# A forgetting bias built by VectorE, modulation sums placed inside dense matmuls, and later turns in a two-block transformer kernel

## Chip, cores and metric

One core of a Trainium2 chip runs the whole program. The metric is the device time of one execution in microseconds (us): 2219.46 us is the median of three runs of the kernel before (2216.54 to 2219.74).

## What is computed

256 tokens of width 2048 pass through two blocks, all in float32. The first block modulates its input with six vectors that come from a conditioning vector `c`, mixes tokens with a two-dimensional Fourier transform, and ends with a squared-ReLU MLP. The second has three kinds of attention heads over one wide projection and another MLP.

```python
# block 1
sh1, sc1, g1, sh2, sc2, g2 = split(silu(c) @ w_mod + b_mod)
h = rms_norm(x, g0) * (1 + sc1) + sh1
x = x + g1 * rms_norm(real(fft2(h per group of 256)) @ fnet_w_out, g1n)
x = x + g2 * rms_norm(relu(h2 @ w_mlp_in)**2 @ w_mlp_out, g3n)      # h2 = norm(x)*(1+sc2) + sh2
# block 2: xn = rms_norm(x) @ w_in gives gq gk gv gg ga fq fk fv fg ff mq mg
gla_o: gated linear attention, decay from ga        (8 heads of 64)
fox_o: logits = q.k/sqrt(d) + c[t] - c[s], causal, softmax, @ v;  c = cumsum(log_sigmoid(ff + b))
mem_o: softmax(mq . mk) @ mv over 256 memory tokens
x = x + (rms_norm([gla_o, fox_o, mem_o]) * gate) @ w_out
x = x + relu(rms_norm(x) @ w_up)**2 @ w_down
```

## The kernel before

**Weights.** Every large weight comes by a 512 KB transfer issued on SP's queue (`load`, L275, in the first part; `ring_group`, L312, later) into a slot of `raw`. The first part uses 12 slots, the rest 8. A float32 weight tile is split into a high part `wh` (ScalarE, `hi`, L949) and a low part `wl` (VectorE, `lo`, L1326), which is written over the raw tile. A "chunk" is one such tile: eight chunks make a group with its own PSUM banks. `T_chunk` (L443 to L449) puts out features on partitions, `N_chunk` (L461 to L463) tokens; a narrow T chunk has 24 matmuls of 256 columns, an N chunk 12 of 512. Matmuls of a chunk wait for `w_lo`; a slot is loaded again only when the chunk in it was used (`chunk_used`). Each engine runs its list of instructions in the order in which the program writes it, so where a step stands in that list is the schedule.

**Block 1, first stages.** The tiles of `w_mod` are multiplied by silu(c) in two ways: four at a time on TensorE (`mod_rows`, L509), or one at a time on VectorE (`gemv`, L1351), and `fold` (L1361) adds the first kind to the second. The result lies spread over 128 partitions in `acc`; `mod_sum` (L518) sums it over partitions with 16 matmuls (32 records) that have a column of ones, one column wide, as their moving operand. The order on TensorE is: the rows of sc1 mixed with Fourier transforms of token halves (`dft_tokens`, L538) and turns of `mem`; then eight T chunks and eight N chunks of the memory projection (`G_MEM`), with sh1's rows between them, `mod_sum(0, 2)` behind chunk 2, `dft_tokens(6)` behind chunk 3 and `dft_tokens(7)` behind the first N chunk; then `mod_sum(1, 7)` and eight `dft_features` (L606 to L608) with g1's rows; then 32 N chunks of `fnet_w_out` beside the gemvs of sc2.

**Start of the first MLP.** The rows of sh2 and the residual come first; `transposes(1, ...)` turns h, ScalarE writes it into `x1t` (L1091), `mod_sum(2, 6, (0,))` gives the first half of sh2, ScalarE adds it for the first two rounds of four tiles (L1099) and VectorE writes their low parts (`shifted_lo`, L1556). Rounds 2 and 3 need the second half: VectorE does the gemvs 24 to 31 with the split of chunk 3 before number 28, TensorE does `mod_sum(2, 7, (1,))` behind chunk 3 of the group (`shift_rest`), and rounds 2 and 3 go before the split of chunk 4. Chunk 4 needs round 2.

**Block 2.** Twelve groups of `w_in` (`WIN_GROUPS`: gq, gk, gv, gv, fq, fk, fv, mq, gg, gg, fg, mg; k = 0 to 11). Beside them, at fixed chunks i, stand the small attention steps. Nine decay levels (`att_level`, L799) serve the gated linear attention: in groups 2 to 5 the even one stands behind chunk 3 and the odd one behind chunk 6, and VectorE has to prepare each (`lvl_pre`, last step L1798). In group 8 `att_qk` computes the forgetting logits behind chunk 3: per head and token half one matmul of q and k, and two matmuls of rank 4 that add c[t] and subtract c[s]:

```python
last = mm(o, qq[:, hd, tb * P:(tb + 1) * P], kk[:, hd, :], start=tb == 0, stop=not fox, ...)      # L827
if fox:
    mm(o, fc[32:36, tb * P:(tb + 1) * P], sel[32:36, hd:hd + 1].to_broadcast([4, S]), ...)        # L830
    last = mm(o, nsel[32:36, hd, :], fc[32:36, :], start=False, stop=True, ...)                   # L832
```

VectorE then does `soft` (L1814 adds the causal mask, L1818 the row maxima, L1821 and L1823 the division; ScalarE the exponentials at L1236), which in its list stands behind the eight splits of group 8 (chunks 4 to 7 of group 8 and 0 to 3 of group 9). `att_turn` (L840) transposes the probabilities behind chunk 0 of group 9 and `att_pv` (L848) follows behind chunk 4. The same steps for the memory heads stand in groups 10 and 11, with no bias: their q·k matmuls are also at L827. `fc`, the running sum of the log forget gates, is ready on partitions 32 to 35 in group 1 (L1882).

Of the kernel before, what the change touches and what calls it, by code (L numbers as in the profile page):

```python
# [27 lines left out]
F32 = mybir.dt.float32  # L28
# [6 lines left out]
P = 128  # L35
# [34 lines left out]
def program(nc, x, c, w_mod, b_mod, norm_g, w_mlp_in, w_mlp_out, fnet_w_out, mem, attn_g, w_in, gla_w2, gla_b,  # L70
            fox_b, fox_qg, fox_kg, mem_g, w_mem_kv, mem_qg, mem_kg, out_g, w_out, mlp_g, w_up, w_down,
            k_ident, k_dft, k_mask, k_nsel, k_sel, k_levels, out):
    ctx = ExitStack()
    with ctx:
# [48 lines left out]
        rbc = at("rbc", [P, S], F32, O_RAW + RAW * 4 * KB)  # L123
        zt = at("zt", [P, 4, S], F32, O_RAW + RAW * 4 * KB + 1 * KB)
# [25 lines left out]
        nsel = at("nsel", [64, 4, P], F32, O_SLOT + 2 * KB)  # L150
# [6 lines left out]
        sel = const("sel", [64, 4], F32)  # L157
# [12 lines left out]
        mv_dram = nc.dram_tensor("mv_spill", [P, HALVES * GC], F32).ap()  # L170
        h_dram = nc.dram_tensor("h_spill", [P, HALVES * D], F32).ap()
# [181 lines left out]
        def _(pool):  # L353
# [59 lines left out]
            pool.dma_start(nsel[32:36, :, :], k_nsel.rearrange("p (a s) -> p a s", a=4)).then_inc(sem("att_const"), 16)  # L413
# [8 lines left out]
            pool.dma_start(flat(mv[:, :, :]), mv_dram).then_inc(sem("mkv_in"), 16)  # L422
            pool.wait_ge(sem("mem_pv"), 1)
# [5 lines left out]
        def _(pe):  # L429
            mm = nc.tensor.matmul  # L430

            def T_chunk(G, i, wide, s, split):
# [3 lines left out]
                for t in range(2):  # L436
                    kt = 2 * i + t
                    for j in range(4):
# [6 lines left out]
                        else:  # L445
# [3 lines left out]
                            last = mm(o, b, xt[:, kt, 0, :], start=False, stop=end, skip_group_check=True)  # L449
                last.then_inc(sem("chunk_used"), 1)  # L450
# [64 lines left out]
            def mod_sum(a, bank, halves=(0, 1)):  # L515

                for kt in range(8 * halves[0], 8 * halves[-1] + 8):
                    last = mm(ps[:, bank, kt:kt + 1], (acc[0], acc[1], acc2)[a][:, kt * P:(kt + 1) * P], ones[:, 0:1], start=True, stop=True,  # L518
                              skip_group_check=True)
                last.then_inc(sem("mod_mm"), 1)  # L520
# [9 lines left out]
            def dft_tokens(g):  # L530
                if g >= 2:
                    pe.wait_ge(sem("tok_out"), g if g == 7 else g - 1)
                for dt in range(2):
# [26 lines left out]
            mod_rows("sc1", C_SC1, 24, 0)  # L560
            pe.wait_ge(sem("rows_folded"), 2)
# [7 lines left out]
            for i in range(CH):  # L569
                if i % 2 == 0:  # L570
                    pe.wait_ge(sem("xt_ready"), 1 + i // 2)
                T_chunk(G_MEM, i, False, *early(i))
# [5 lines left out]
                if i == 2:  # L578
                    pe.wait_ge(sem("const_set"), 2)
                    mod_sum(0, 2)  # L580
            for i in range(CH):
# [4 lines left out]
                if i == 0:  # L586
                    dft_tokens(7)
# [265 lines left out]
            for k, (name, off) in enumerate(WIN_GROUPS):  # L853
                G = G_WIN + k
                bank_free(G)
                for i in range(CH):
# [17 lines left out]
                    if 2 <= k <= 5 and i == 6:  # L874
                        att_level(2 * (k - 2) + 1)
# [1147 lines left out]
```

## Time and profile before

| | |
|---|---|
| median of 3 runs | 2219.46 us |
| the profiled execution, its own time | 2221.41 us |
| its span, first to last instruction | 2219.7 us |
| TensorE matmul / weight load busy | 2156.7 us (97%) / 1823.6 us (82%) |
| VectorE / ScalarE / GpSimd busy | 1324.4 us (60%) / 972.6 us (44%) / 45.2 us (2%) |
| granted TensorE clock, mean | 0.98 of full |
| chain that ended last | TensorE 90%, VectorE 4%, DMA 3%, ScalarE 2% |

TensorE is busy nearly always, but busy does not mean fast: matmuls overlap in the pipeline, and where the granted clock is 0.50 each takes twice as long and counts as busy all the same. So three things are to be read of TensorE: its work, its waits and its clock. The execution's own time is 1.7 us over its span.

### The profile page before, as it was taken

To read this page: it belongs to the slowest core of one execution; us is meant where nothing else is said; L and a number is where in the kernel's file an instruction comes from. 1 tells how busy PE (TensorE), PEld (TensorE's weight loads), DVE (VectorE), ACT (ScalarE), POOL (GpSimd) and SP (SyncE) were. 2 spreads that over 40 slices of the span, in tenths; PEclk is the share of its full clock that TensorE was granted. 3 is DMA by queue.
4 is the path that set the end of the run, shared out by engine and by line. 5 is a ranking of instruction groups with operands and counts; after the bars stand their busy time and mean duration, and the time that the engine had idled before them with its cause. 6 is when DMAs were issued, how large, how long until landed. Compare 5 with 4: busy or idle time off the path is not lost.

```text
span 2219.7 us, 31332 instructions
## 1 busy us (share of the span) xinstructions
PE 2156.7 (97%) x11753; PEld 1823.6 (82%) x11753; DVE 1324.4 (60%) x1318; ACT 972.6 (44%) x1134; POOL 45.2 (2%) x69
## 2 busy tenths in 40 slices
PE   5999988999999999999999999999999999999999
PEld 3867867888888888888979879888888888888887
DVE  3568976655655565656766547655645554655563
ACT  4244435343434443434534446754534343443342
POOL 0000000000000000001000000000000000000000
PEclk9889989999999999999999989999999999999999
DMA  9899996667667667666655535556656656656654
GB/s 388 287 404 347 390 372 203 210 220 214 209 213 214 211 213 219 207 210 206 209 145 151 145 97 145 198 185 186 192 191 190 187 192 189 188 190 190 188 189 151
DMA packets 219188, 478.98 MB, mean 216 GB/s; under 512 B 14708, under 2 KB 15084, under 8 KB 218336
## 3 DMA queue, kind: packets, MB, share of 16 engines
q1 hardware_dynamic: 211940, 450.98, 63.0%
q0 software_dynamic: 6480, 25.69, 3.7%
q8 instruction: 60, 0.98, 0.2%
q10 hardware_dynamic: 684, 1.14, 0.1%
q14 instruction: 24, 0.20, 0.0%
HBM read 472.50 MB, written 5.24 MB: 215 GB/s over the span
## 4 chain that ended last, share of the span: by engine, by line
PE 90%; DVE 4%; DMA 3%; ACT 2%; issue 1%; SPq 0%; DVEq 0%; ACTq 0%
PE ps L443 21%; PE ps L461 13%; PE ps L463 13%; PE ps L462 13%; PE ps L444 11%; PE ps L447 3%; PE ps L448 3%; PE ps L449 3%; DMA raw<-in_w_mod_dram 1%; DVE acc L1351 1%; PE ps L509 1%; DMA raw<-in_w_in_dram 1%; PE ps L487 1%; DVE wl L1326 1%; PE ps L799 1%
## 5 line engine op out<-in xcount | busy, mean ns | idle before, releaser
L1326 DVE TENSOR_TENSOR wl<-raw,wh 128x1024 fp32r<-128x1024 f32 x688 | 812.2, 1220 | 333.2 <-ACT wh L949 332.1
L949 ACT ACTIVATE wh<-raw 128x1024 fp32r<-128x1024 f32 x688 | 699.8, 1054 | 539.1 <-DMA raw<-in_w_down_dram 161.5
L443 PE MATMUL ps<-xt,wh 128*128 128x512 f32 x2048 | 724.8, 399 | 9.0 <-DVE wl L1326 9.0
L444 PE MATMUL ps<-xt,wl 128*128 128x256 f32 x2048 | 576.2, 281 | 0.0
L443 PEld LDWEIGHTS ps<-xt,wh 128*128 128x128 f32 x2048 | 386.1, 189 | 105.5 <-issue 10.7
L461 PE MATMUL ps<-wh,u 128*128 128x512 f32 x1120 | 436.7, 390 | 0.3 <-DVE wl L1326 0.3
L462 PE MATMUL ps<-wl,u 128*128 128x512 f32 x1120 | 435.8, 389 | 0.0
L463 PE MATMUL ps<-wh,u 128*128 128x512 f32 x1120 | 435.8, 389 | 0.0
L444 PEld LDWEIGHTS ps<-xt,wl 128*128 128x128 f32 x2048 | 388.6, 190 | 0.3
L461 PEld LDWEIGHTS ps<-wh,u 128*128 128x128 f32 x1120 | 210.2, 188 | 44.9 <-issue 0.8
L463 PEld LDWEIGHTS ps<-wh,u 128*128 128x128 f32 x1120 | 210.2, 188 | 43.8
L462 PEld LDWEIGHTS ps<-wl,u 128*128 128x128 f32 x1120 | 210.2, 188 | 43.5 <-issue 0.2
L447 PE MATMUL ps<-xt,wh 128*128 128x256 f32 x640 | 188.1, 294 | 5.2 <-DVE wl L1326 4.0
L448 PE MATMUL ps<-xt,wh 128*128 128x256 f32 x640 | 184.5, 288 | 0.0
L449 PE MATMUL ps<-xt,wl 128*128 128x256 f32 x640 | 184.4, 288 | 0.0
L1606 DVE TENSOR_TENSOR tmp<-ps,tmp 128x1024 f32<-128x1024 f32 x32 | 39.2, 1225 | 172.6 <-ACT tmp L1124 172.6
L447 PEld LDWEIGHTS ps<-xt,wh 128*128 128x128 f32 x640 | 126.3, 197 | 10.5 <-issue 9.7
L448 PEld LDWEIGHTS ps<-xt,wh 128*128 128x128 f32 x640 | 126.3, 197 | 1.1 <-issue 1.0
L449 PEld LDWEIGHTS ps<-xt,wl 128*128 128x128 f32 x640 | 126.2, 197 | 0.0
L1124 ACT ACTIVATE tmp<-ps 128x1024 f32<-128x1024 f32 x32 | 32.9, 1027 | 201.0 <-PE ps L444 201.0
L461 PE MATMUL ps<-wh,xt 128*128 128x512 f32 x256 | 102.7, 401 | 4.2 <-DVE wl L1326 4.2
L1351 DVE SCALAR_TENSOR_TENSOR acc<-raw,siluc,acc 128x1024 f32<-128x1024 f32 x80 | 102.3, 1280 | 5.0 <-DMA raw<-in_w_mod_dram 1.9
(287 smaller groups left out, 1579.3 us busy)
## 6 DMA issues: line engine op xcount, KB each, us to landing
raw<-in_w_mod_dram SPq DMA_DIRECT2D x160, 512.0 KB, 8.1
raw<-in_w_mlp_in_dram SPq DMA_DIRECT2D x128, 512.0 KB, 3.8
raw<-in_w_mlp_out_dram SPq DMA_DIRECT2D x128, 512.0 KB, 4.7
raw<-in_w_up_dram SPq DMA_DIRECT2D x128, 512.0 KB, 3.8
raw<-in_w_down_dram SPq DMA_DIRECT2D x128, 512.0 KB, 3.7
raw<-in_w_in_dram SPq DMA_DIRECT2D x96, 512.0 KB, 3.7
raw<-in_fnet_w_out_dram SPq DMA_DIRECT2D x32, 512.0 KB, 5.2
slot<-in_w_mod_dram POOLq DMA_DIRECT2D x32, 512.0 KB, 4.7
```

The source lines that it names most:

```text
L443: mm(o, a, flat(xt[:, kt, :, :]), start=first, stop=end, skip_group_check=True)
L444: last = mm(o[:, 0:S], b, xt[:, kt, 0, :], start=False, stop=end, skip_group_check=True)
L447: mm(o, a, xt[:, kt, 0, :], start=first and j % 2 == 0, stop=False, skip_group_check=True)
L448: mm(o, a, xt[:, kt, 1, :], start=False, stop=False, skip_group_check=True)
L449: last = mm(o, b, xt[:, kt, 0, :], start=False, stop=end, skip_group_check=True)
L461: mm(o, hi, wh[:, i, t, :], start=kt == 0, stop=False, skip_group_check=True)
L462: mm(o, hi, wl[:, s, t, :], start=False, stop=False, skip_group_check=True)
L463: last = mm(o, lo, wh[:, i, t, :], start=False, stop=kt == KT - 1, skip_group_check=True)
L949: A(flat(wh[:, i, :, :]), raw[:, landed[0], :], ACT.Copy).then_inc(sem("w_hi"), 1)
L1326: V.tensor_tensor(flat(wl[:, s, :, :]), raw[:, s, :], flat(wh[:, i, :, :]).bitcast(F32), ALU.subtract).then_inc(sem("w_lo"), 1)
L1351: V.scalar_tensor_tensor(out=t, in0=raw[:, s, :], scalar=siluc[:, kt:kt + 1], in1=t, op0=ALU.mult, op1=ALU.add).then_inc(mod_used(mod_c(c0 ...
L1606: V.tensor_tensor(tmp[:, :, :], ps[:, b0:b0 + 4, 0:S], tmp[:, :, :], ALU.add).then_inc(sem("evacuated"), 1)
```

## The change

1. Forgetting bias. The rank-4 matmuls go, with `sel` and `nsel` and their two constant loads. GpSimd's queue writes `fc` to DRAM, reads it back as a row repeated on all partitions (`fcb`, 512 KB) and as columns (`fcq`, 1024 elements of 4 bytes), and VectorE builds `bias` = (mask + c[t]) - c[s] with eight instructions at the end of group 7. `soft` adds `bias` in place of `mask`. `rbc` and `zt` move to other addresses.
2. `att_turn("fox")` moves from behind chunk 0 to behind chunk 1 of group 9.
3. The odd decay levels move from behind chunk 6 to behind chunk 7.
4. `mod_sum(0, 2)` is spread in pairs between the matmuls of memory chunk 3. 14 matmuls of the identity (`keep_busy`) are issued before the first memory chunk.
5. `dft_tokens(7)` moves behind the memory groups, and `mod_sum(1, 7)` is spread in pairs between its matmuls; ScalarE copies its result (`tok_out(7)`) later, and `mod_rows("g1", ..., 16)` waits for that.
6. First MLP: the first half of sh2's sum goes to bank 2 and ahead of the wait for `x1t`, the second half goes from behind chunk 3 to behind chunk 2, and on ScalarE and VectorE the splits of the first chunks and the shifted tiles are put in another order, with rounds 2 and 3 between the splits of chunks 4 and 5. ScalarE's first quarter is written out instead of looped.

```diff
@@ tensor engine
-            def T_chunk(G, i, wide, s, split):
+            def T_chunk(G, i, wide, s, split, beside=None):
...
+                        if beside:
+                            beside(4 * t + j)
...
+            def sum_pair(a, bank):
+
+                def pair(n):
+                    mod_sum(a, bank, kts=(2 * n, 2 * n + 1), end=n == KT // 2 - 1)
+                return pair
...
-            def dft_tokens(g):
+            def dft_tokens(g, beside=None):
...
+                            n += 1
+                            if beside and n < KT // 2:
+                                beside(n)
...
             mod_rows("sc1", C_SC1, 24, 0)
+            pe.wait_ge(sem("xt_ready"), 4)
+            keep_busy(14, 3)
             pe.wait_ge(sem("rows_folded"), 2)
...
-                T_chunk(G_MEM, i, False, *early(i))
+                if i == 3:
+                    pe.wait_ge(sem("const_set"), 2)
+                T_chunk(G_MEM, i, False, *early(i), beside=sum_pair(0, 2) if i == 3 else None)
...
-                if i == 2:
-                    pe.wait_ge(sem("const_set"), 2)
-                    mod_sum(0, 2)
...
-                if i == 0:
-                    dft_tokens(7)
...
             pe.wait_ge(sem("rows_folded"), 4)
-            mod_sum(1, 7)
+            pe.wait_ge(sem("mk_ln"), 1)
+            dft_tokens(7, sum_pair(1, 7))
             pe.wait_ge(sem("evacuated"), 2)
             mod_rows("g1", C_G1, 0, 2)
-            pe.wait_ge(sem("mk_ln"), 1)
...
-            pe.wait_ge(sem("x1t_out"), 4)
             pe.wait_ge(sem("rows_folded"), 7)
-            mod_sum(2, 6, (0,))
             pe.wait_ge(sem("evacuated"), G_ML1)
+            mod_sum(2, 2, (0,))
+            pe.wait_ge(sem("x1t_out"), 3)
             mod_rows("sh2", C_SH2, 16, 4)
...
-                if i == HEAD - 1:
+                if i == HEAD - 2:
                     pe.wait_ge(*mod_used(mod_c(C_SH2, MODN - 1)))
+                    pe.wait_ge(sem("x1t_out"), 4)
                     mod_sum(2, 7, (1,))
...
-                        last = mm(o, qq[:, hd, tb * P:(tb + 1) * P], kk[:, hd, :], start=tb == 0, stop=not fox,
-                                  skip_group_check=True)
-                        if fox:
-                            mm(o, fc[32:36, tb * P:(tb + 1) * P], sel[32:36, hd:hd + 1].to_broadcast([4, S]),
-                               start=False, stop=False, skip_group_check=True)
-                            last = mm(o, nsel[32:36, hd, :], fc[32:36, :], start=False, stop=True, skip_group_check=True)
+                        last = mm(ps[:, 4 + hd, tb * S:(tb + 1) * S], qq[:, hd, tb * P:(tb + 1) * P], kk[:, hd, :],
+                                  start=tb == 0, stop=True, skip_group_check=True)
...
-                    if 2 <= k <= 5 and i == 6:
+                    if 2 <= k <= 5 and i == 7:
                         att_level(2 * (k - 2) + 1)
...
-                    if (k, i) == (9, 0):
+                    if (k, i) == (9, 1):
                         att_turn("fox", pf)
@@ gpsimd
+            pool.wait_ge(sem("fc_ready"), 1)
+            pool.dma_start(fc_dram, fc[32:36, :]).then_inc(sem("fc_out"), 16)
+            pool.wait_ge(sem("fc_out"), 16)
+            pool.dma_start(flat(fcb[:, :, :]), fc_dram.rearrange("h s -> (h s)").rearrange("(o n) -> o n", o=1)
+                           .to_broadcast([P, 4 * S])).then_inc(sem("fc_in"), 16)
+            pool.dma_start(fcq[:, :].rearrange("p (h t) -> p h t", h=4),
+                           fc_dram.rearrange("h (t p) -> p h t", p=P), allow_slow_non_contiguous=True).then_inc(sem("fc_in"), 16)
             pool.wait_ge(sem("mem_pv"), 1)
@@ scalar engine
+            hi_static(CH * G_ML1)
+            hi_static(CH * G_ML1 + 1)
+            shifted_hi(0)
+            shifted_hi(1)
+            hi_static(CH * G_ML1 + 2)
+            hi_static(CH * G_ML1 + 3)
+
+            def shift_rest(j):
+
+                if j == 1:
+                    shifted_hi(2)
+                    shifted_hi(3)
@@ vector engine
-                if m == 5:
+                if m == 6:
                     mod_vector(1, vtmp[:, :], 2)
...
+            lo_static(CH * G_ML1)
             shift_half(0)
-            for r in range(2):
-                shifted_lo(r)
-                lo_static(CH * G_ML1 + r)
+            shifted_lo(0)
+            lo_static(CH * G_ML1 + 1)
+            shifted_lo(1)
             lo_static(CH * G_ML1 + 2)
             for n in range(24, 32):
                 if n == 25:
                     fold("sh2", C_SH2, 1, 2, 4)
-                if n == 28:
-                    lo_static(CH * G_ML1 + 3)
                 gemv("sh2", C_SH2, n, 2)
-            shift_half(1)
-            for r in (2, 3):
-                shifted_lo(r)
+            lo_static(CH * G_ML1 + 3)
+
+            def shift_rest(j):
+
+                if j == 1:
+                    shift_half(1)
+                    shifted_lo(2)
+                    shifted_lo(3)
...
-                    link(V.tensor_tensor(dst, src, flat(mask[:, :, :]).rearrange("p (o n) -> p o n", o=1)
-                                         .to_broadcast([P, 4, 2 * S]), ALU.add))
+                    link(V.tensor_tensor(dst, src, banks(bias[:, :, :], 4), ALU.add))
...
                     scale_heads(fk, lambda j: v("fkg"), fksq[:, :, :], 4).then_inc(sem("fox_qk_ready"), 1)
+                    dve.wait_ge(sem("att_const"), 16)
+                    dve.wait_ge(sem("fc_in"), 32)
+                    for j in range(8):
+                        last = V.scalar_tensor_tensor(out=bias[:, j, :], in0=mask[:, j % 2, :], scalar=fcq[:, j:j + 1],
+                                                      in1=fcb[:, j // 2, :], op0=ALU.add, op1=ALU.subtract)
+                    link(last)
```

## Rows read from the trace of the kernel before

**Rows 1.** Busy time by stretch: from:to, length, then each engine, granted clock, DMA share, GB/s.
```profile
70.00:110.00 40.00, 40.00 (x273) 36.19 (x274) 22.84 (x21) 8.38 (x9) 2.29 (x2) 0.84 0.85 298
110.00:150.00 40.00, 37.23 (x185) 26.26 (x187) 24.92 (x24) 17.47 (x20) 1.10 (x2) 0.93 1.02 400
150.00:200.00 50.00, 45.30 (x301) 33.13 (x294) 39.89 (x84) 22.47 (x43) 2.86 (x3) 0.86 0.96 367
200.00:290.00 90.00, 88.59 (x407) 73.58 (x405) 81.84 (x77) 34.14 (x44) 3.64 (x4) 1.00 1.01 380
290.00:350.00 60.00, 45.38 (x268) 32.63 (x268) 44.79 (x56) 29.25 (x53) 2.07 (x3) 0.80 0.83 309
```

**Rows 2.** Waits of TensorE over the whole span: us in total, times, longest.
```profile
PE ps L443 <- DVE wl L1326: 9.0, 3, 6.6
...
PE ps L799 <- DVE kd L1798: 5.6, 4, 1.8
...
PE ps L447 <- DVE wl L1326: 4.0, 1, 4.0
```

**Rows 3.** TensorE's groups by form: the forgetting logits, and the memory heads' q·k.
```profile
L830 PE MATMUL ps<-sel,fc 4*128 4x256 f32 x16 | 8.1, 597 | 0.0
...
L827 PE MATMUL ps<-fk,fq 128*128 128x256 f32 x16 | 7.6, 566 | 0.0
L832 PE MATMUL ps<-fc,nsel 4*128 4x256 f32 x16 | 7.0, 533 | 0.0
...
L827 PE MATMUL ps<-mk,mq 128*128 128x256 f32 x16 | 3.6, 379 | 0.0
```

**Rows 4.** Busy time by stretch again, cut where the granted clock changes.
```profile
69.00:75.80 6.80, 5.88 (x28) 5.91 (x29) 3.89 (x4) 1.06 (x1) 0.00 (x0) 0.50 1.00 352
...
86.00:92.80 6.80, 6.80 (x33) 6.80 (x33) 3.52 (x5) 1.79 (x2) 2.29 (x2) 0.50 1.02 387
...
147.50:157.70 10.20, 9.02 (x43) 5.98 (x43) 8.23 (x20) 1.71 (x4) 2.31 (x2) 0.50 1.03 404
297.40:305.00 7.60, 7.58 (x64) 7.27 (x64) 6.13 (x5) 4.71 (x12) 0.00 (x0) 1.00 1.03 404
...
1157.80:1161.20 3.40, 3.40 (x24) 2.98 (x21) 0.00 (x0) 0.00 (x0) 0.00 (x0) 0.50 0.10 40
...
1297.70:1318.20 20.50, 20.50 (x56) 13.70 (x57) 5.99 (x5) 1.16 (x5) 0.00 (x0) 0.50 0.00 1
1318.20:1329.20 11.00, 11.00 (x94) 11.00 (x93) 4.75 (x11) 5.29 (x15) 0.00 (x0) 1.00 0.65 179
```

**Rows 5.** Timeline of TensorE, 1291 to 1331 us: start, length, what.
```profile
1291.98 0.60 PE L827 MATMUL ps<-fk,fq 128*128 128x256 f32 x2
...
1329.26 1.91 PE L840 MATMUL ps<-ident,pf 128*128 128x128 f32 x16
```

**Rows 6.** Timeline of VectorE, 1289 to 1324 us.
```profile
1289.78 9.16 DVE L1326 TENSOR_TENSOR wl<-raw,wh 128x1024 fp32r<-128x1024 f32 x8
1312.18 2.29 DVE L1814 TENSOR_TENSOR pf<-ps,mask 128x2048 f32<-128x2048 f32 x1 [13.25 <-PE ps L832]
...
1321.36 2.19 DVE L1823 TENSOR_SCALAR pf<-pf,rs 128x256 f32<-128x256 f32 x8
```

**Rows 7.** Timeline of VectorE, 321 to 341 us.
```profile
321.03 1.22 DVE L1361 SCALAR_TENSOR_TENSOR acc<-ps,acc 128x1024 f32<-128x1024 f32 x1 [1.13 <-PE ps L509]
...
326.34 1.22 DVE L1326 TENSOR_TENSOR wl<-raw,wh 128x1024 fp32r<-128x1024 f32 x1
327.47 5.45 DVE L1351 SCALAR_TENSOR_TENSOR acc<-raw,siluc,acc 128x1024 f32<-128x1024 f32 x4
...
336.99 3.26 DVE L1556 SCALAR_TENSOR_TENSOR xt<-x1t,s,xt 128x256 fp32r<-128x256 f32 x8 [1.87 <-ACT xt L1099]
```

**Rows 8.** Timeline of TensorE at 83 us: the first partition sum.
```profile
83.22 4.30 PE L518 MATMUL ps<-ones,acc 128*128 128x1 f32 x32
```

**Rows 9.** Narrow loads on GpSimd's queue into `wsr`, 16 and 4 columns of 2048 rows.
```profile
DMA to landing us min/median/max: 6.8/6.9/7.0
```

More of the change, by code:

```diff
@@ L149, in program @@
         mask = at("mask", [P, HALVES, S], F32, O_SLOT)
-        nsel = at("nsel", [64, 4, P], F32, O_SLOT + 2 * KB)
+        fcq = at("fcq", [P, 8], F32, O_SLOT + 3 * KB)
+        fcb = at("fcb", [P, 4, S], F32, O_RAW + RAW * 4 * KB + 4 * KB)
+        bias = at("bias", [P, 8, S], F32, O_RAW + RAW * 4 * KB + 8 * KB)
         ident = const("ident", [P, P], F32)
@@ L513, in mod_rows, with mod_sum, keep_busy @@
                             last.then_inc(mod_used(cc)[0], 1)
-            def mod_sum(a, bank, halves=(0, 1)):
-                for kt in range(8 * halves[0], 8 * halves[-1] + 8):
+            def sum_pair(a, bank):
+                def pair(n):
+                    mod_sum(a, bank, kts=(2 * n, 2 * n + 1), end=n == KT // 2 - 1)
+                return pair
+            def mod_sum(a, bank, halves=(0, 1), kts=None, end=True):
+                for kt in kts or range(8 * halves[0], 8 * halves[-1] + 8):
                     last = mm(ps[:, bank, kt:kt + 1], (acc[0], acc[1], acc2)[a][:, kt * P:(kt + 1) * P], ones[:, 0:1], start=True, stop=True,
                               skip_group_check=True)
-                last.then_inc(sem("mod_mm"), 1)
+                if end:
+                    last.then_inc(sem("mod_mm"), 1)
+            def keep_busy(n, bank):
+                for _ in range(n):
+                    mm(ps[:, bank, 0:P], ident[:, :], ident[:, :], start=True, stop=True)
             def keep_busy(n, bank):
@@ L620, in _ @@
                     n = G1_ROWS_AT[g]
+                    if n == KT:
+                        pe.wait_ge(sem("tok_out"), 8)
                     mod_rows("g1", C_G1, n, 2 if n < KT else 4)
@@ L1036, in _ @@
             act.wait_ge(sem("a1_ready"), 1)
-            act.wait_ge(sem("tok_out"), 8)
+            act.wait_ge(sem("tok_out"), 7)
             def p_hi(g):
+                if g == 7:
+                    act.wait_ge(sem("tok_out"), 8)
                 if g < 2:
@@ L1058, in _ @@
                     p_hi(g + 1)
+                if g == 0:
+                    tok_out(7)
                 fm_hi(g)
@@ L1094, in _, with shifted_hi @@
             act.wait_ge(sem("x1t_out"), 4)
-            for r in range(4):
+            def shifted_hi(r):
                 act.wait_ge(sem("a2_ready"), 2 + r // 2)
@@ L1115, in out_hi, with mlp_quarter @@
                 return step
-            def mlp_quarter(G0, ups, q, first=False, last=False):
+            def mlp_quarter(G0, ups, q, first=None, last=False):
                 def up(p, e, between=None):
@@ L1130, in mlp_quarter @@
                         for e in range(2):
-                            up(p, e, out_hi(GQ - 1) if p == 0 and e == 0 else None)
+                            up(p, e, first if p == 0 and e == 0 else None)
                 else:
@@ L1158, in mlp_quarter @@
                             down(p, e)
-            with act.Fori(0, QT - 1) as q:
+            mlp_quarter(G_ML1, 0, 0, first=shift_rest)
+            with act.Fori(1, QT - 1) as q:
                 mlp_quarter(G_ML1, 0, q)
@@ L1305, in _ @@
                       accum_out=ssq[:, a, g:g + 1]).then_inc(sem("osqs"), 1)
-            mlp_quarter(G_ML2, 4 * QT, 0, first=True)
+            mlp_quarter(G_ML2, 4 * QT, 0, first=out_hi(GQ - 1))
             with act.Fori(1, QT - 1) as q:
@@ L1547, in shift_half @@
                 k8 = slice(8 * half, 8 * half + 8)
-                V.tensor_copy(s2[:, k8], ps[:, 6 + half, k8]).then_inc(sem("a2_ready"), 1)
+                V.tensor_copy(s2[:, k8], ps[:, 7 if half else 2, k8]).then_inc(sem("a2_ready"), 1)
                 dve.wait_ge(sem("a2_ready"), 2 + half)
```

32 lines of the change are left out of this document (12 added, 20 removed).

## Prediction

> **What bounds the kernel.** I read the page first: TensorE busy 97% and 90% of the chain, so only TensorE's own time, its waits and its clock count, except where transfers limit it. Then the table by stretch, to see which. In the mean the transfers are at 0.85 of their capacity from 70 to 110 us, at 1.02 from 110 to 150, at 0.96 from 150 to 200 and at 1.01 while `fnet_w_out` and sc2 come in, up to 290 us [rows 1]. The reader should see that TensorE's gains ahead of 290 us are worth only what they let the transfers start sooner. From 350 us on the change touches only places in block 2. Third, the waits: the largest that the change aims at are the first MLP's chunk behind its splits, 9.0 us in three (6.6 the longest), the decay levels behind VectorE, 5.6 us in four, and the first memory chunk, 4.0 us [rows 2]. Fourth, the groups: the forgetting logits' three lines sum to 8.1 + 7.6 + 7.0 = 22.7 us, where the memory heads' same q·k costs 3.6 [rows 3]. Last, the stretches at half clock (1.2 instead of 2.4 GHz) [rows 4].
>
> **Forgetting logits: the largest term.** Before, they start at 1291.98 and the turn starts at 1329.26, five chunks later [rows 5]. They drag the clock to 0.50 from 1297.7 to 1318.2, into the chunks behind them [rows 4]. At full clock 94 chunk matmuls take 11.00 us [rows 4], so a chunk of 24 takes 2.8 us. The later turn's place would have come at 1329.26 + 2.8 = 1332.1 with the old code. After: 16 q·k matmuls at the memory heads' price, 3.5 us [rows 3], end at 1295.5, and six chunks, 16.9 us, end at 1312.4. Then TensorE wants the probabilities. VectorE: the bias is eight instructions on 128x256 operands in SBUF, and eight such (`shifted_lo`) took 3.26 us [rows 7]. They push the eight splits (9.16 us from 1289.78 [rows 6]) to 1302.3. Behind them comes `soft`, which took 1321.36 + 2.19 - 1312.18 = 11.4 us including ScalarE's exponentials [rows 6], so 1313.7. TensorE waits 1.3 us and turns at 1313.7: 1332.1 - 1313.7 = **18.4 us** gained. The cover of the bias was the long run of rank-4 matmuls, and it is gone. The split of chunk 4 is then done at 1289.8 + 3.3 + 1.2 = 1294.3 and wanted at 1295.5; a microsecond of slack is left. Ends: 19.7 if `soft` is in time, 14 if something of ScalarE's or VectorE's work between slips by 4.5 us, half of `soft`. Behind the turn, VectorE has the copy and the gates, and three more chunks (8.4 us) stand before the product with v, against four before; I charge nothing for it, and the 14 covers it.
>
> **The new transfers** are issued on GpSimd's queue in group 1, where `fc` becomes ready, so well before the slow stretch of the levels at 1157.8 [rows 4], and wanted at 1290: at least 132 us. The narrow loads of the old kernel landed in 7.0 us at most [rows 9]; three such in a row are 21 us. Behind them on that queue stands only the reload of h, for after the memory heads. Cost zero, to at most 1 us by delaying a tile of `w_in`.
> The Trainium skill, "DMA: Bandwidth & Descriptors", Rules for kernel authors, says that a last dimension that isn't contiguous becomes one descriptor per element, so 1024 for `fcq`; no row here shows a transfer of 4-byte pieces, and it would have to land 19 times later than the narrow ones to matter.
>
> **Decay levels.** Moved one chunk (2.8 us) later, against waits of at most 1.8 us [rows 2], all four vanish: 5.6 us. The 1.8 us wait also led to 3.4 us at half clock [rows 4], worth 1.7. VectorE finds the level's result a little later at the group's end, and the next even level is a chunk and more away. **7.0 us**, between 4 (new waits of 0.4 us each at chunk 7, the clock lost again) and 7.3.
>
> **First stages.** `keep_busy` fills the 4.0 us wait [rows 2], whose end the fold and the split of chunk 0 set, so it delays nothing; chunks 0 and 1 should then run at full clock instead of half for 5.9 busy us [rows 4], 2.9 us. `mod_sum` takes 4.30 us for 32 records [rows 8], and the clock falls behind it for 6.8 us [rows 4], worth up to 3.4; between dense matmuls I keep the 4.3 us and save the clock. The second sum is the same and has 10.2 us at half clock behind it [rows 4], worth up to 4.5 on 9.0 busy us. `dft_tokens(7)` only changes place. TensorE's own gain is thus near 10 us, but the transfers move the same bytes: they stood idle 0.15 x 40 = 6.0 us from 70 to 110 and 0.04 x 50 = 2.0 from 150 to 200 [rows 1], and nearly none otherwise. No more than about 8 can come through; new waits for tiles take a little of it: **7.5 us**, between 3 (the clock still falls at both sums, and only the start and small pieces remain) and 9.
> Is a pair of one-column matmuls in a stream of dense ones dense enough for the clock? The turns of h, 64 matmul records of 128 columns in 7.6 us, kept it at 1.00 [rows 4]; the rank-4 matmuls did not, and the sums alone do not. The mixture lies between. I take the turns as nearer, since the dense matmuls have all rows and columns.
> The Trainium skill, "TensorE: Matmul & The Clock Gate", "Part 2: What happens when you issue a matmul", says that the weights of the next matmul load while this one runs; with its 107 ns for 128 columns, 16 hidden loads would be an estimated 1.7 us less TensorE work than I count. The trace's sum alone, 134 ns per record [rows 8], agrees that weight loads set its pace. It would change the sum by nothing, as the transfers cap the term.
>
> **Start of the first MLP.** Old order: fold at 321.03, three gemvs, split of chunk 3 (1.2 us), four gemvs to 332.9, sum, copy, ScalarE's and VectorE's rounds from 336.99 to 340.25, split of chunk 4, chunk 4 at about 341.5 [rows 7]. New: the first half's sum need not wait for the last turned tiles and the split of chunk 0 stands ahead, so chunk 0 and with it the fold come sooner; of L443's 9.0 us of waits, 2.4 lie in two shorter ones [rows 2], and I take 2.0 of them as gone. Without the split the gemvs end at 332.9 - 2.0 - 1.2 = 329.7. From their end to VectorE's rounds the sum, a copy and ScalarE's round took 336.99 - 332.9 = 4.1 us [rows 7], and VectorE's round 2 is half of 3.26, so round 2 is ready at 329.7 + 4.1 + 1.6 = 335.4, with chunk 4's split already done. Chunk 3 now stands behind the sum (half of 4.30 us [rows 8]) and beside the rounds: it ends at 331.8 + 2.8 = 334.6, or 337 if TensorE's wait for the gemvs (about 5 us, new) costs it the clock. So chunk 4 starts between 335.5 and 337 instead of 341.5: **5.0 us**, ends 2 and 7. What is late next is the split of chunk 5, behind rounds 2 and 3.
>
> **Sum.** 18.4 + 7.0 + 7.5 + 5.0 = 37.9 us. Span 2219.7 - 37.9 = 2181.8; the execution's own time 2221.4 becomes 2183.5; it lies 1.9 us over the median of the runs, so I give 2219.46 - 37.9 = 2181.6 us.
>
> **Rivals.** (a) VectorE becomes the bound in groups 8 and 9: splits, bias, softmax and gates all stand in one list, and the turn waits 5 us more than I say: 2187 us. For: the slack ahead of chunk 4 falls to a microsecond. Against: VectorE stood idle 13.25 us before `soft` [rows 6], more than the bias adds. (b) The clock falls in the mixed sums, or the turned order only shifts the waits for tiles: the first stages give 2 to 3 us: 2186.5 us. For: transfers at 1.02 behind 110 us [rows 1]. (c) Both parts ahead of 350 us are absorbed by transfers: only block 2 counts, 25.4 us: 2194 us. Against: transfers stand at 0.83 from 290 to 350 [rows 1]. (d) Slower: `fcq`'s pieces land so late that VectorE stands at the bias and holds all splits of group 8. It decides only when the landing comes 132 us or more after the issue, and every microsecond from there costs one, so slower than before needs a landing of 132 + 38 = 170 us or more, against 7.0 [rows 9]; say 2225 us. (e) More than I say: `soft` in time, all clocks kept: 2176 us.
>
> **Chances.** Forecast as summed, with its small errors (2178 to 2185): 0.58. (a) 0.13, (b) 0.15, (c) 0.06, (d) 0.02, (e) 0.06. The range takes in (a), (b) and (e), and most of (c): 2174 to 2194. A measurement of this kernel can tell about 0.2% (4.4 us) from no change; all cases but (d) are faster by more: faster 0.97, same 0.01, slower 0.02.
>
> **What would show it.** L830 and L832 gone and L827 for fk at 3.6 us; a wait of about 1.3 us at the turn behind VectorE; no wait of L799; granted clock 1.00 at 70 to 93 us and in 1290 to 1318; the waits of L443 in the first MLP at some 3 us in place of 6.6, and a new one of about 5 us behind L1351 ahead of its second sum. It would be wrong with a wait for `fc_in`, a clock of 0.50 in memory chunk 3, or `fnet_w_out`'s stage starting less than 5 us sooner.

## The result, and the profile after

The changed kernel takes 2191.45 us in the median of four runs (2189.92 to 2193.19), against 2219.6 for the kernel before beside it: ratio 0.9872, 95% interval 0.9860 to 0.9884. The profiled execution is its lowest, 2189.92 us with a span of 2187.9; that of before was 2221.4, above its own median. The spans differ by 31.8 us, the medians by 28.

The table by stretch of the changed kernel, columns as in [rows 1], and below it the stretches cut at the clock, to be held against [rows 4]:

```profile
70.00:110.00 40.00, 39.59 (x293) 34.17 (x293) 24.14 (x22) 10.35 (x11) 2.29 (x2) 1.00 0.95 351
110.00:150.00 40.00, 34.41 (x169) 22.01 (x168) 28.15 (x33) 17.31 (x23) 3.40 (x4) 0.92 0.99 389
150.00:200.00 50.00, 43.38 (x304) 32.04 (x301) 38.01 (x77) 21.82 (x40) 0.55 (x1) 0.96 0.91 348
200.00:290.00 90.00, 89.55 (x414) 72.51 (x412) 82.80 (x76) 35.22 (x47) 5.70 (x6) 0.98 1.02 385
290.00:350.00 60.00, 49.96 (x293) 39.50 (x290) 43.59 (x56) 28.48 (x52) 0.54 (x1) 0.82 0.87 317
...
69.00:75.80 6.80, 6.16 (x53) 6.00 (x51) 3.81 (x4) 1.06 (x1) 0.00 (x0) 1.00 0.99 352
80.00:88.00 8.00, 8.00 (x69) 7.86 (x68) 3.98 (x4) 2.12 (x2) 0.00 (x0) 1.00 1.02 393
138.00:147.00 9.00, 8.12 (x49) 6.82 (x52) 6.84 (x9) 3.08 (x6) 2.23 (x2) 0.82 1.03 421
1157.80:1161.20 3.40, 3.40 (x31) 3.40 (x30) 3.40 (x5) 3.40 (x5) 0.00 (x0) 1.00 0.71 210
1297.70:1318.20 20.50, 19.80 (x144) 18.22 (x143) 18.26 (x22) 16.11 (x18) 0.00 (x0) 1.00 0.47 129
```

Block 2 has no stretch at half clock any more. The first memory chunks and the first mixed sum (80 to 88) are at 1.00. But look at the transfers: from 70 to 110 us their idle share fell from 0.15 to 0.05, and from 150 to 200 it rose from 0.04 to 0.09. TensorE's waits, columns as in [rows 2]:

```profile
PE ps L631 <- DVE pdft L1512: 6.5, 2, 3.5
...
PE ps L471 <- DVE wl L1364: 5.7, 8, 1.9
PE ps L534 <- DVE acc L1389: 5.3, 1, 5.3
PE ps L451 <- issue: 2.6, 1, 2.6
...
PE ps L863 <- DVE pf L1864: 0.7, 1, 0.7
```

The waits of the decay levels (before's L799, now L827) are gone. So are two of the three waits of the first MLP's chunks (L443, now L451), the 6.6 us one among them. The third, of chunk 0, is still there: 2.6 us under the label "issue", against 1.5 before. The wait ahead of the second sum (L534) is 5.3 us, as forecast, and the one for the feature DFT's table (L631) is 6.5. Neither is quite new; before they were

```profile
PE ps L606 <- DVE pdft L1474: 4.7, 2, 3.5
...
PE ps L518 <- DVE acc L1351: 2.3, 1, 2.3
```

Of the two waits for the table, the one of 3.5 us is as before. The other was 1.2 us at 153 us and is now 2.9 us at 189.

**Where the time went.** I took the start of the same TensorE group in every trace at five places of the kernel (times of before): a turn of y at 56.70, the turns of h at 297.41, block 2's first turns at 1042.73, the last q·k behind the levels at 1232.09, and the forgetting heads' product with v at 1342.51. The lead over the trace of before, differenced from place to place, gives each part its own number. In us, positive is sooner; "median" is the median's distance from that of before beside it:

```
kernel                      start  first stages  MLP start  levels  forgetting  median
forecast                             7.5           5.0       7.0     18.4       37.9
changed                     -0.2     3.6           2.7       7.1     18.5       28.2
e1_fox_alone                 0.3     0.0           0.1      -0.5     18.5       19.2
e2_levels_at_6              -1.2    -0.1           4.3      -3.6     18.5       20.5
e3_first_stages_old          0.3     1.7           2.5       7.1     18.5       30.0
e4_mlp_start_old             1.6     5.5          -1.4       6.8     18.5       27.0
e5_after_again               1.6     3.9           3.3       7.0     18.5       27.6
e6_dft7_old                  0.0     4.7           3.5       6.9     18.5       32.9
e7_scaling_ahead_of_tiles    0.0     4.9           3.3       6.9     18.5       33.2
e8_busy_before_second_sum    0.2     1.7           4.6       7.1     18.5       32.3
e9_four_edits                0.1     8.2           7.8       7.1     18.5       39.1
e10_turn_at_0                1.9     1.1           2.8       6.8     14.0       27.1
e11_plain_first_sum          0.1    -1.6           3.6       7.2     18.5       27.6
e12_copy_first              -1.6    -0.3           5.0       6.7     18.5       30.2
```

The levels and the forgetting heads repeat to a few tenths. The first stages don't: seven traces with exactly the changed kernel's first stages (changed, e2, e4, e5, e8, e10, e12) lie between -0.3 and 5.5, mean 2.2. The old first stages scatter too: 0 in before by definition, 0.0 in e1, 1.7 in e3. A single profile can't price that part, and a gain of 2.2 is measured from one trace of before.

### The profile page after: what moved, and what is told of

It is laid out like the page before. It is cut to its first block, busy times and chain, and to the rows that moved or that the text cites. A ratio compares the mean times of both kernels' runs of the same rounds, so it can differ in the third digit from the quotient of the medians.

```text
span 2187.9 us, 31310 instructions
## 1 busy us (share of the span) xinstructions
PE 2133.3 (98%) x11749; PEld 1806.7 (83%) x11749; DVE 1328.4 (61%) x1326; ACT 974.1 (45%) x1134; POOL 46.5 (2%) x71
## 4 chain that ended last, share of the span: by engine, by line
PE 90%; DVE 4%; DMA 3%; ACT 1%; issue 1%; SPq 0%; DVEq 0%; ACTq 0%
PE ps L451 22%; PE ps L471 14%; PE ps L473 13%; PE ps L472 13%; PE ps L452 11%; PE ps L455 3%; PE ps L457 3%; PE ps L456 3%; DMA raw<-in_w_mod_dram 2%; PE ps L519 1%; DVE acc L1389 1%; PE ps L827 1%; DVE wl L1364 1%; DMA raw<-in_w_mem_kv_dram 1%; PE ps L561 1%
## 5 line engine op out<-in xcount | busy, mean ns | idle before, releaser
L451 PE MATMUL ps<-xt,wh 128*128 128x512 f32 x2048 | 726.6, 399 | 2.6 <-issue 2.6
L451 PEld LDWEIGHTS ps<-xt,wh 128*128 128x128 f32 x2048 | 386.5, 189 | 100.2 <-issue 5.2
L455 PE MATMUL ps<-xt,wh 128*128 128x256 f32 x640 | 185.0, 289 | 1.9 <-issue 1.2
L456 PE MATMUL ps<-xt,wh 128*128 128x256 f32 x640 | 181.0, 283 | 0.0
L455 PEld LDWEIGHTS ps<-xt,wh 128*128 128x128 f32 x640 | 122.7, 192 | 5.8 <-issue 5.0
L456 PEld LDWEIGHTS ps<-xt,wh 128*128 128x128 f32 x640 | 122.7, 192 | 1.1 <-issue 1.0
```

Source lines behind the costliest of these rows:

```text
L451: mm(o, a, flat(xt[:, kt, :, :]), start=first, stop=end, skip_group_check=True)
L455: mm(o, a, xt[:, kt, 0, :], start=first and j % 2 == 0, stop=False, skip_group_check=True)
L456: mm(o, a, xt[:, kt, 1, :], start=False, stop=False, skip_group_check=True)
```

## The experiments

**The forgetting bias alone** (e1): the kernel before with the transfers of `fc`, the bias and the later turn.

```diff
 kernel before, with only:
+ fc_dram, fcb, fcq and their transfers; bias on VectorE
- rank-4 matmuls in att_qk; turn at (9, 0)
+ turn at (9, 1)
```

> The kernel before with the forgetting bias on VectorE and the later turn alone; decay levels, first stages and the MLP's start as before. My theory: this term is independent of the rest and worth 18.5 us, 13.24 us being the lead of the changed kernel ahead of group 7's sums and 31.8 behind the turn; time 2219.5 - 18.5 = 2201 us, and the trace shows a wait of 0.5 to 1.5 us at the turn. Rival: part of the 18.5 us belongs to the levels (the clock, or VectorE's list reaching the bias sooner), so the term alone gives 14 us or less: 2205.5 or more. Half clock in the fox part would be a sign of the rival.

2201.81 us against 2221.0 (ratio 0.9912, 0.9898 to 0.9926), 18.5 us in the trace and a wait of 0.7 us at the turn: the term is right and stands alone. The changed kernel's VectorE timeline shows the working:

```profile
1276.53 3.25 DVE L2002 SCALAR_TENSOR_TENSOR bias<-mask,fcq,fcb 128x256 f32<-128x256 f32 x8
1279.81 9.17 DVE L1364 TENSOR_TENSOR wl<-raw,wh 128x1024 fp32r<-128x1024 f32 x8
1288.90 2.29 DVE L1856 TENSOR_TENSOR pf<-ps,bias 128x2048 f32<-128x2048 f32 x1
...
1298.08 2.19 DVE L1864 TENSOR_SCALAR pf<-pf,rs 128x256 f32<-128x256 f32 x8
```

The bias runs without a wait for its transfers, eight splits follow, `soft` takes 1300.27 - 1288.90 = 11.4 us. With the lead of 13.2 us added, the turn is ready at 1313.5; the forecast said 1313.7. `fcq` landed in

```profile
DMA to landing us min/median/max: 5.7/5.7/5.7
```

and `fcb` in 5.0. By the rule of the Trainium skill, "DMA: Bandwidth & Descriptors", Rules for kernel authors, its 1024 elements are as many descriptors; the trace shows no price for that here (the narrow loads of 16 columns took 6.9 [rows 9]).

**The levels back behind the seventh chunk** (e2).

```diff
-                    if 2 <= k <= 5 and i == 7:
+                    if 2 <= k <= 5 and i == 6:
                         att_level(2 * (k - 2) + 1)
```

> The changed kernel with the odd decay levels back behind the seventh chunk. My theory: the four waits (1.3, 1.8, 1.1, 1.4 us) and the 3.4 us of half clock return, so 7.0 us slower than the changed kernel: span 2187.9 + 7.0 = 2194.9 us. Rival: the waits come from the transfers of w_in and only move, so they would show elsewhere in the changed kernel and undoing costs 3 us or less.

2200.45 us, 20.5 under before; in the trace 7.1 + 3.6 = 10.7 us more than the changed kernel. TensorE's waits from 1080 to 1245 us, its clock around the first of them, and the ScalarE split that was late for it:

```profile
PE ps L827 <- DVE kd L1840: 7.3, 4, 3.1
```

```profile
1120.00:1135.00 15.00, 11.92 (x69) 9.97 (x68) 5.51 (x7) 2.12 (x2) 0.00 (x0) 0.89 0.38 105
```

```profile
1120.52 1.06 ACT L971 ACTIVATE wh<-raw 128x1024 fp32r<-128x1024 f32 x1 [3.39 <-DMA raw<-in_w_in_dram]
```

All four waits are back, the first 3.1 instead of 1.3 us, since ScalarE stood 3.4 us for one tile of `w_in` ahead of it, and that wait has half clock behind it too. The changed kernel has nearly the same late tile (2.95 us) and doesn't feel it. So the move is worth 7, and more where a tile is late. The medians agree: 20.5 under before, where the changed kernel is 28.2 and 27.6 under in its two measurements. The rival is out.

**The first stages as before** (e3) and **the first MLP's start as before** (e4), each in the changed kernel.

```diff
 e3, in the changed kernel:
- keep_busy(14, 3); mod_sum(0, 2) and mod_sum(1, 7) in pairs beside a chunk and beside dft_tokens(7)
+ mod_sum(0, 2) behind chunk 2, mod_sum(1, 7) by itself, dft_tokens(7) behind N chunk 0
 e4, in the changed kernel:
- hi_static(0, 1), shifted_hi(0, 1); one block of gemvs; second half of the shift inside the first pass of `up`
+ the order, the banks and the waits of before
```

> The changed kernel with the first stages as before (no keep_busy, both whole sums between the memory chunks, the last token DFT behind the fifth chunk). My reading of the two traces: they carry 3.4 us to the end of fnet_w_out's stage, so 3.4 us slower than the changed kernel, span 2191.3 us. Rival A: the start of the first MLP takes up what the first stages lose or gain (transfers bound both), so no slower than 1 us. Rival B: the prediction's 7.5 us was right and the MLP's start gave less, so 7 us slower.

> The changed kernel with the first MLP's start in the old order. My reading of the two traces: this part is worth 2.7 us beyond the lead it inherits, so span 2190.6 us. Rival: it is worth the predicted 5.0 us (then 2192.9) and the lead of the first stages is lost in it; the lead at the last partition sum of fnet_w_out's stage would be 3.4 us in both cases, only the chunks behind 350 us tell them apart.

e3: 2191.03 us, 30.0 under before (0.9863, 0.9847 to 0.9879). That is no slower than the changed kernel (0.9872, and 0.9880 in e5): the whole part on the first stages brings nothing that the medians can tell. That is rival A's number, but not its mechanism, as the MLP's start gave its usual 2.5 us. e4: 2194.02 us, 27.0 under before. In its trace the old start lost 1.4 us of a lead of 7.2, where the new one gains 3.3 in the mean of eight traces (2.5 to 4.3), so by the traces the new start is worth 3 us or a little more. The medians don't show that much: e4 lies 0.6 us nearer to before than e5 and 1.2 nearer than the changed kernel, and the intervals are wider than 3 us.

**The changed kernel again** (e5).

> The changed kernel, unaltered, on the same chip as the next three. The traces so far have the same code of the first stages in three kernels, and its lead over the trace of before at the turns of h was 3.4, -1.3 and 7.2 us. My theory: the first 300 us run at the rate of the transfers, which scatters between executions, so this profile has yet another lead, between -1.5 and 7.5 us; behind the forgetting turn the lead is 25.6 us more than ahead of block 2, within 0.3. Rival: the scatter is a property of each kernel, then the lead is again 3.4 within 0.3 us.

2192.35 us against 2219.92 (0.9880, 0.9863 to 0.9896). Its lead at the turns of h is 5.5 us, where the first profile had 3.4, and from block 2 to the product with v it gains 34.30 - 8.83 = 25.5. So the scatter belongs to the executions, not to the kernels. What makes it was not tried.

**The last token DFT back in its place** (e6), and **ScalarE's scalings ahead of the next stage's tiles** (e7).

```diff
 e6, in the changed kernel:
                 N_chunk(G_MEM + 1, i, xt, False, *early(CH + i))
                 sh1_rows(CH + i)
+                if i == 0:
+                    dft_tokens(7)
...
-            dft_tokens(7, sum_pair(1, 7))
+            mod_sum(1, 7)
 (and ScalarE's tok_out(7) and the waits for it as before)
 e7, in the changed kernel:
-                if g in (5, 6):
-                    hi_static(CH * G_FN + 2 * (g - 5))
-                    hi_static(CH * G_FN + 2 * (g - 5) + 1)
+                if g in (6, 7):
+                    hi_static(CH * G_FN + 2 * (g - 6))
+                    hi_static(CH * G_FN + 2 * (g - 6) + 1)
```

> The changed kernel with the last token DFT back behind the fifth memory chunk and the second whole sum by itself; keep_busy and the first mixed sum stay. My theory: moving the DFT uncovered 2.8 us of waits for tiles behind it (5.6 us of waits from 115 to 139 us against 2.8 before), and the mixed sum keeps the clock for only part of its time, so this kernel is the same as the changed one within 1 us. Rival: the clock held by the mixed sum is worth the predicted 4.5 us less the waits, so this kernel is 2 to 4 us slower.

> The changed kernel with ScalarE's four splits of fnet_w_out's first tiles behind its last scaling of the DFT (p_hi of group 7) instead of ahead of it. My theory: the 2.9 us wait of TensorE for the feature DFT at 189 us is ScalarE standing at a tile that hasn't landed (1.3, 1.6 us), so it goes; but the same tiles are wanted by fnet_w_out's first chunks 15 us later, and the transfers have no idle time there, so at most 1 us of it comes through. Rival: the wait was ScalarE's order alone, 2.5 to 3 us come through.

Both expectations were too low. e6: 2187.01 us (0.9852, 0.9834 to 0.9871), 5.3 under e5; e7: 2186.77 (0.9854, 0.9832 to 0.9876), 5.6 under. Each of these intervals overlaps that of e5, and the near 5 us that each has in the first stages lie inside the scatter of the seven traces, so the size of either gain is open. The waits say more. From 95 to 145 us TensorE waits 3.8 us in e6, 4.6 to 5.9 in the seven traces (5.9 in the changed kernel, of which 0.9 is the mixture's own wait for the fold, at L561) and 2.8 before. For e7, this is what ScalarE did in the changed kernel, and the wait of TensorE that came of it:

```profile
181.41 1.06 ACT L971 ACTIVATE wh<-raw 128x1024 fp32r<-128x1024 f32 x1 [1.29 <-DMA raw<-in_fnet_w_out_dram]
184.01 1.06 ACT L971 ACTIVATE wh<-raw 128x1024 fp32r<-128x1024 f32 x1 [1.55 <-DMA raw<-in_fnet_w_out_dram]
184.98 0.49 ACT L1069 ACTIVATE pdft<-praw,a 128x255 fp32r<-128x255 f32 x1
```

```profile
189.19 0.39 PE L631 MATMUL ps<-pdft,dfth 128*128 128x256 f32 x1 [2.94 <-DVE pdft L1512]
```

The label names VectorE. But VectorE had stood for ScalarE's table (L1069), and ScalarE for two tiles that only the next stage wants. Once TensorE was sooner, this list was too early for the transfers. The wait at 189 us is in all seven traces (1.8 to 4.0 us) and in e6 and e11 (2.2 and 2.1), and in none with the old first stages (before, e1, e3) or with this edit (e7, e9). In e7 the waits of 150 to 200 us are

```profile
PE ps L631 <- DVE pdft L1512: 3.5, 1, 3.5
```

and the first chunk of `fnet_w_out` waits 0.8 us, against 0.45 in the changed kernel. I had expected the tile's wait to come back there, and it didn't.

**Idle matmuls ahead of the second sum** (e8).

```diff
                 if i == HEAD - 2:
-                    pe.wait_ge(*mod_used(mod_c(C_SH2, MODN - 1)))
                     pe.wait_ge(sem("x1t_out"), 4)
+                    keep_busy(20, 6)
+                    pe.wait_ge(*mod_used(mod_c(C_SH2, MODN - 1)))
                     mod_sum(2, 7, (1,))
```

> The changed kernel with 20 idle matmuls (keep_busy) in TensorE's 5.3 us wait for the gemvs ahead of the second sum of the first MLP's shift. My theory: the clock fell because of that wait, so the sum takes 2.2 instead of 3.6 us and chunk 3 takes 2.9 instead of 4.1, and chunk 4, which then waits for VectorE's third round, starts 1.5 to 2.5 us sooner: about 2190 - 2 us. Rival: chunk 4 is bound by VectorE's rounds and the splits anyway, nothing is gained.

In the changed kernel, 322 to 338 us and its second sum:

```profile
322.00:338.00 16.00, 10.70 (x49) 9.44 (x48) 12.31 (x18) 7.45 (x13) 0.00 (x0) 0.68 0.79 279
```

```profile
327.79 3.58 PE L534 MATMUL ps<-ones,acc 128*128 128x1 f32 x16 [5.30 <-DVE acc L1389]
```

In e8:

```profile
322.00:338.00 16.00, 13.94 (x99) 12.56 (x98) 13.54 (x19) 7.26 (x13) 0.00 (x0) 1.00 0.97 342
```

```profile
329.38 1.95 PE L534 MATMUL ps<-ones,acc 128*128 128x1 f32 x16 [0.90 <-DVE acc L1390]
335.37 0.50 PE L451 MATMUL ps<-xt,wh 128*128 128x512 f32 x1 [1.16 <-DVE xt L1595]
```

The clock stays at 1.00, the sum takes 1.95 instead of 3.58 us, and chunk 4 now waits 1.2 us for VectorE's rounds. The start of the MLP gives 4.6 us instead of 3.3, so 1.3, just under the expected 1.5. 2187.66 us (0.9853, 0.9837 to 0.9870).

**The copy of the shift first** (e12).

```diff
-            hi_static(CH * G_ML1)
-            hi_static(CH * G_ML1 + 1)
             shifted_hi(0)
+            hi_static(CH * G_ML1)
+            hi_static(CH * G_ML1 + 1)
             shifted_hi(1)
...
-            lo_static(CH * G_ML1)
             shift_half(0)
             shifted_lo(0)
+            lo_static(CH * G_ML1)
+            shifted_lo(1)
             lo_static(CH * G_ML1 + 1)
-            shifted_lo(1)
```

> The changed kernel with the copy of the shift's first half and the first round on ScalarE ahead of the splits of chunks 0 and 1. My theory: VectorE's copy stood 2.2 us behind a finished sum because the split of chunk 0 was ahead of it, so chunk 0 starts 4.9 instead of 6.2 us after that sum's end, and the gemvs, the second sum and chunk 4 come 1.3 us sooner. Rival: the split then comes late by as much, and chunk 0 starts no sooner.

VectorE in the changed kernel, where the first half's sum was done at 301.41 + 1.84 = 303.25:

```profile
304.30 1.23 DVE L1364 TENSOR_TENSOR wl<-raw,wh 128x1024 fp32r<-128x1024 f32 x1 [3.75 <-ACT wh L971]
305.45 0.16 DVE L1586 COPY s<-ps 128x8 f32<-128x8 f32 x1
307.70 1.67 DVE L1594 SCALAR_TENSOR_TENSOR xt<-x1t,s,xt 128x256 fp32r<-128x256 f32 x4 [2.10 <-ACT xt L1126]
```

and its TensorE at chunk 0

```profile
309.48 0.77 PE L451 MATMUL ps<-xt,wh 128*128 128x512 f32 x1 [2.63 <-issue]
```

The chunk starts as VectorE's first shifted tiles end (307.70 + 1.67 = 309.37), so that is what it waited for behind the label "issue"; e2, e5 and e10, with the same code here, name L1594. In e12, VectorE and then TensorE:

```profile
308.64 0.17 DVE L1586 COPY s<-ps 128x8 f32<-128x8 f32 x1 [2.74 <-PE ps L534]
```

```profile
306.76 1.84 PE L534 MATMUL ps<-ones,acc 128*128 128x1 f32 x16
...
313.70 0.47 PE L451 MATMUL ps<-xt,wh 128*128 128x512 f32 x1 [0.86 <-DVE wl L1364]
```

The copy follows the sum at once, and chunk 0 starts 313.70 - 308.60 = 5.1 us behind the sum's end instead of 309.48 - 303.25 = 6.2. The part gives 5.0 instead of 3.3 us, where 1.3 more was expected; the unedited start reached 4.3 in one trace (e2), so the 1.1 us between the two places is the surer number. 2190.89 us (0.9862, 0.9847 to 0.9877).

**The first sum as one block** (e11).

```diff
-                T_chunk(G_MEM, i, False, *early(i), beside=sum_pair(0, 2) if i == 3 else None)
+                T_chunk(G_MEM, i, False, *early(i))
...
+                if i == 2:
+                    pe.wait_ge(sem("const_set"), 2)
+                    mod_sum(0, 2)
```

> The changed kernel with the first whole sum between memory chunks 2 and 3 as one block instead of inside chunk 3; keep_busy and the rest stay. My theory: the block brings the clock down, so the stretch from the end of chunk 2 to the end of chunk 3 takes 9.4 us as before instead of 6.4 (lead ahead of the sixth token DFT 3 us smaller), and two thirds of that or less are left at the turns of h. Rival: with the first memory chunks at full clock the clock survives one block of sums, and the stretch takes 4.3 + 2.9 = 7.2 us.

Its memory chunks 0 and 1, and the block with chunk 3 behind it:

```profile
69.00:76.00 7.00, 6.36 (x54) 5.98 (x57) 3.81 (x4) 1.06 (x1) 0.00 (x0) 1.00 1.01 350
80.00:90.60 10.60, 10.60 (x73) 10.23 (x72) 4.59 (x4) 2.62 (x3) 0.00 (x0) 0.84 1.03 398
```

```profile
80.58 3.63 PE L534 MATMUL ps<-ones,acc 128*128 128x1 f32 x32
84.07 0.36 PE L455 MATMUL ps<-xt,wh 128*128 128x256 f32 x1
```

Sum and chunk take 88.52 - 80.58 = 7.9 us, against 9.4 before (83.22 to 92.65) and 6.4 mixed: between the two theories. The clock does fall behind the block, but for less of the chunk. The block itself, at full clock, takes 84.07 - 80.58 = 3.5 us. With a chunk of 2.8 us that makes 6.3, as much as the mixture takes, so mixing saves nothing but the clock. The lead at the sixth token DFT is 1.6 us smaller (4.1 - 0.1 against 5.5 + 0.2 in the changed kernel); its first stages give the least of all, -1.6. 2193.51 us (0.9872, 0.9857 to 0.9887).

**The turn in its old place** (e10).

```diff
-                    if (k, i) == (9, 1):
+                    if (k, i) == (9, 0):
                         att_turn("fox", pf)
```

> The changed kernel with the turn of the forgetting probabilities at its old place, a chunk earlier. With the turn at the new place TensorE waits 0.7 us. My theory: here it waits 0.7 + 2.8 = 3.5 us, the chunk (2.8 us) then runs behind it, and the end comes only as much later as the clock costs that the wait brings down: the lead behind the product with v falls by 2.8 (the wait that nothing covers) to 5 us. Rival: the probabilities come sooner because VectorE has no chunk's split ahead of them, then the wait is under 2 us and nothing is lost.

```profile
PE ps L863 <- DVE pf L1864: 3.6, 1, 3.6
```

That is the wait of 0.7 plus the chunk of 2.8 us, and 18.5 - 14.0 = 4.5 us of the lead are lost, inside the expected 2.8 to 5. 2193.92 us (0.9877, 0.9862 to 0.9892): the median shows only 0.5 to 1.1 us of the loss against the two measurements of the changed kernel, and its interval is too wide to tell that from 4.5.

**Four edits together** (e9): e6, e7, e8 and e12.

> The changed kernel with the edits of the last call that were not slower, together (last token DFT at its old place, ScalarE's scalings ahead of the tiles of fnet_w_out, 20 idle matmuls ahead of the second sum) and with the copy of the first half of the shift ahead of the split of chunk 0. My theory: the gains lie in different waits and mostly add, 1 to 2 us each in the traces, so 4 to 6 us under the changed kernel's median: 2186 or less against a before of 2220. Rival: the transfers cap all of them together, then it is no better than the single edits, 2187.

2181.95 us (2179.8 to 2183.09) against 2221.06, ratio 0.9825, 0.9812 to 0.9839: faster than both kernels, 39 us under before where the changed one is 28 under. Its TensorE waits, by the same view:

```profile
PE ps L633 <- DVE pdft L1510: 5.7, 4, 3.5
PE ps L471 <- DVE wl L1362: 3.9, 5, 1.9
PE ps L451 <- DVE wl L1362: 2.9, 1, 2.9
...
PE ps L534 <- DVE acc L1387: 0.8, 1, 0.8
```

and its stretches:

```profile
150.00:200.00 50.00, 45.70 (x303) 33.86 (x303) 44.79 (x84) 22.67 (x42) 1.09 (x3) 0.97 0.98 370
...
290.00:350.00 60.00, 55.98 (x358) 47.79 (x357) 47.63 (x54) 32.49 (x52) 0.53 (x1) 0.94 0.89 317
```

From 150 to 200 us the transfers are at 0.98, where the changed kernel has 0.91. The first stages give 8.2 us and the MLP's start 7.8, both outside what the unedited code gave in any trace, and more than the single edits promised.

## Why the prediction was right in direction and too high in size

- **Forgetting logits**, 18.4: 18.5, in all twelve traces that have it with the later turn, and alone in e1. q·k takes the forecast 3.6 us; the turn waits 0.7 instead of 1.3 us. The later turn is part of it: without it 14.0. **New transfers**, 0: 0. No wait for them, and the late tile behind them costs nothing in the changed order; that they delayed it was not tried.
- **Decay levels**, 7.0: 6.7 to 7.2, all waits and the stretch at half clock gone.
- **First stages**, 7.5: 2.2 in the mean, 3.6 in the first profile. This is the term that failed, and two sentences of it. "`dft_tokens(7)` only changes place": at its old place it covered waits, and moved back it leaves 3.8 us of them between 95 and 145 us instead of 4.6 to 5.9; at the new one, behind such waits, the mixture is not all at full clock (0.82 from 138 to 147). "New waits for tiles take a little of it": in the changed kernel the waits from 95 to 145 us grew from 2.8 to 5.9 us and those for the DFT's table from 4.7 to 6.5, together 4.9, more than half of the 7.5. The second kind comes through ScalarE's list, in which tiles of the next stage stand ahead of the last scaling. The rest of the working held: memory chunks 0 and 1 at full clock and the first mixture at 1.00. The cap of about 8 us from the transfers' idle time fits the 8.2 of e9, in which both placings are mended, but one trace doesn't prove a cap. Rival (b) gave 2 to 3 us, and its second cause, shifted waits, is what came; its first, a clock that falls in the mixed sum, holds for the second sum only. The prediction's own sign of being wrong came as well: `fnet_w_out`'s stage starts at 195.20 instead of 197.67 us, 2.5 us sooner, not 5. Half clock is a little cheaper than "twice as long": in memory chunk 3 before, matmuls start every 0.21 us at 0.50, and every 0.12 us at 1.00 in chunk 2.
- The Trainium skill, "TensorE: Matmul & The Clock Gate", "Part 2: What happens when you issue a matmul", on weights that load while a matmul runs: the prediction estimated from it that 1.7 of the 4.3 us counted would be hidden. Sum and chunk mixed take 6.4 us, 3.5 more than a chunk, but that is no hidden load. The same sum as one block at full clock takes 3.5 us as well (e11), and the 4.30 of before ran into half clock at 86.0 [rows 4]. No run here shows a saving from it.
- **Start of the first MLP**, 5.0: 3.3 in the mean. The wait ahead of the second sum (5.3 for 5) came, and chunk 4's 6.6 us went, where some 3 were expected to stay. "2.0 of them as gone" failed: of the two shorter waits of L443 the later, 0.9 us, went, but chunk 0's own grew from 1.5 to 2.6. It came no sooner behind its sum but 1.1 us later (6.2 us against 5.1), since the split of chunk 0 stands ahead of VectorE's copy (e12 gives 1.7 back in its trace, 1.1 of it at this place), and the clock fell in the longer wait, which I had charged only at the late end of the range (e8 gives 1.3 back).
- **Sum**, 37.9: the parts' means are 18.5 + 7.0 + 2.2 + 3.3 = 31.0. The trace of before lies 1.9 us over its median, which leaves 29.1, against 28.2 and 27.6 in the medians. The forecast of 2181.6 was 10 us too low. The measured time lies inside the range of 2174 to 2194, but outside the 2178 to 2185 that had a chance of 0.58, and the number nearest to it is the 2194 of rival (c), which had 0.06. The size, then, was mostly missed. Rival (c)'s mechanism, that nothing ahead of 350 us comes through, did not hold: the lead at block 2 is 6.1 us in the first profile, and 2.2 to 8.8 in the other traces of the changed kernel or of it with one edit (e2 to e12 without e9). But most of the two parts was lost. Rivals (a) and (d) fell (a turn's wait of 0.7 us, `fcq` in 5.7 us).

## What to carry to other kernels

Where the transfers set the pace, a step that was moved off TensorE's waits isn't moved for nothing: list what it covered, and look in each engine's list for tiles of the next stage that stand ahead of this stage's work. A wait of some microseconds is priced with the clock behind it, and idle matmuls in it give that back. Price a part by leads between fixed places of several traces: one trace was enough for block 2, and off by up to 3.3 us for the first stages.

## What the runs showed that I had not expected

- The same instructions gave leads from -0.3 to 5.5 us over the first 300 us in seven traces, while the levels and the forgetting heads repeated within 0.5 and 0.1 us.
- One-column matmuls in pairs between dense ones kept the clock at 1.00 (80 to 88 us), where the block of the same 16 was followed by 0.50 before [rows 4], and the stretch with it has a mean of 0.84 in e11. The second mixture, with waits of 1.9 and 0.9 us just ahead of it, did not keep it (0.82 from 138 to 147).
- The four edits gave 2.5, 2.7, 1.3 and 1.7 us of lead over the means, 8.2 in sum, and 10.5 together. Their medians lay 5.3, 5.6 and 4.7 us (e6, e7, e8) under that of e5, more than their traces show; with four runs each and overlapping intervals it can be chance. Only the four together are clear of it.
